# Where the split activations begin in memory, relative to the weights, stage by stage

## The chip, the cores and the metric

One core of one Trainium2 chip runs the program. The metric is the device time in microseconds of that core. The kernel before took 2813.97 us (median of 3 runs, 2809.7 to 2837.8). The execution that was profiled took 2824.21 us, with a span of 2822.4 us from its first to its last instruction.

## The reference, cut to what matters

Two models of two layers each run one after the other on a sequence of 256 tokens of width 1024. The first also carries 256 context tokens, except behind the mixer of its last layer. Every layer is feed-forward, mixer, feed-forward; the mixers are windowed attention, differential attention, retention with dilated attention, and a gated linear attention. In shortened form:

```python
def _swiglu(h, w_gate, w_up, w_down):
    return (jax.nn.silu(h @ w_gate) * (h @ w_up)) @ w_down     # 1024 -> 2816 -> 1024
...
hx = hx + 0.5 * mx[:, 2] * _swiglu(_pre(hx, ...), gate, up, down)   # feed-forward
hx = hx + mx[:, 5] * mixer(_pre(hx, ...))                           # w_in, mixing, w_out
hx = hx + 0.5 * mx[:, 8] * _swiglu(_pre(hx, ...), gate, up, down)   # feed-forward
```

There are eight feed-forwards and four mixers, all in float32. The matrix products with weights make up nearly all of the arithmetic.

## The kernel before, in words

Activations lie transposed: the width is on the 128 partitions, in DT = 8 tiles, and the tokens are the columns (256, or 512 with the context). A float32 product with weights is made from three products in the format float32r. The weight piece (128 x 8 tiles x 128) is loaded into `raw`, ScalarE rounds it to `WH` (L1242), and VectorE writes the rest, raw minus WH, to `WL` (L1579). The activation is split in the same way into a high and a low half. For every weight tile, `three` (L738) issues WH times high (L741), WH times low (L742) and WL times high (L743), all adding into one PSUM bank. Each of these matmuls has its own weight load of 128 columns, which runs beside the matmul before it. So while L741 streams the high half, the WH of L742 is being loaded; beside L742 the WL of L743 is loaded, and beside L743 the WH of the next tile.

The halves lie in two large buffers. `x_all` holds the normalised input of a stage: the high half at element `at`, and the low half at `at` plus 4096 elements (`x_view`, L197). A tile of it is 512 elements. In the stages with 256 columns the feed-forward and the input projection of a mixer read the second half of a tile (`x_scaled`, 256 elements = 1024 bytes further on). `h_all` holds the hidden activation of a feed-forward in the same way, with 22 tiles (`h_view`, L218). The rows of `raw`, `WH` and `WL` are 16384 bytes each and that of `x_all` is 33280 bytes, all multiples of 512, and the allocation brings `h_all` onto the same remainder by 512 bytes (`skew` is there for that). A weight tile is 512 bytes. With `at` = 0 every streamed operand therefore begins on the same remainder by 512 bytes as every weight tile, and `at` shifts it from there: 4 bytes for each element.

Three tuples say what `at` is in each stage. `NORM_X` has it for each of the 13 norms, which stand ahead of: feed-forward 0, attention mixer, feed-forward 1 (first layer of the first model), feed-forward 2, differential mixer, feed-forward 3 (second layer), feed-forward 4, retention mixer, feed-forward 5, feed-forward 6, linear-attention mixer, feed-forward 7 (second model), and the output. `MIX_X` has it for what the four mixers hand to their output projection, and `FFN_H` for the hidden activation of the eight feed-forwards. Feed-forwards 0 to 2 and the first mixer have 512 columns, and so have the four key and value iterations of the differential mixer; all else has 256.

A feed-forward is an "up" stage of 1056 matmuls and a "down" stage of 528. The input projections of the mixers have 288, 192 + 384, 672 and 576, the output projections 192 each, which makes 15552 matmuls in all: 5616 with 512 columns and 9936 with 256. SP loads the weights four pieces ahead, and the order of the stages is fixed. The halves are written by ScalarE (high: L1319, L1386, L1333) and VectorE (low: L1732, L1795, L1746).

Of the kernel before, what the change touches and what calls it, by code (L numbers as in the profile page):

```python
# [31 lines left out]
S = 256  # L32
D = 1024
DT = D // P
# [118 lines left out]
def build(nc, A):  # L153
    ctx = ExitStack()
    with ctx:
# [40 lines left out]

        def x_view(at, low):  # L197

            at += DT * 2 * S if low else 0
            return x_all[:, at:at + DT * 2 * S].rearrange("p (k n) -> p k n", k=DT)  # L200

        NORM_X = (0, 0, 0, 0, 0, 112, 112, 112, 112, 112, 112, 112, 0)
        MIX_X = (0, 112, 112, 112)
        FFN_H = (0, 0, 0, 368, 368, 368, 368, 368)
        x_high = lambda at: x_view(at, False)
        x_low = lambda at: x_view(at, True)


# [90 lines left out]
        def add(g):  # L299
            g.s0 = state["scaled"]  # L300
            if g.kind == "up" and g.scale:
                state["scaled"] += g.iters
            g.p0, g.e0, g.r0, g.a0 = state["p0"], state["e0"], state["r0"], state["a0"]
            state["p0"] += g.n * g.iters
            if g.kind == "res":
                state["r0"] += 4 * g.iters
            else:
                state["e0"] += g.iters
            if g.ada is not None:
                state["a0"] += g.iters  # L310
            gemms.append(g)
            steps.append(("gemm", g))
            return g

        def x_in(at):
            return lambda k, t: (x_high(at)[:, k, 0:t], x_low(at)[:, k, 0:t])
# [8 lines left out]
        def norm(t, weight, shift=None, mode="split"):  # L325
# [4 lines left out]
            n["mul0"] = state["mul"]  # L330
            n["x"] = NORM_X[n["i"]]
            n["c0"] = S if t == S else 0
# [23 lines left out]
        def at(name, d):  # L356

            return A[name][bass.ds(d, 1), :, :, :].rearrange("o p k n -> (o p) k n")

        def ffn(n, t, gate, wg, wu, wd, ada=((KH, None),)):  # L360
            ready, hid0, i0 = (lambda k: (n_low, n["h0"] + k + 1)), state["hid"], 0
            h_at = FFN_H[hid0 // FT]
            for iters, tile in ada:
# [31 lines left out]
        def out_proj(w, t, m, gate):  # L395
            return add(Gemm("res", 2, DT, t, lambda i, _, b: at(w, i * 4 + b),
                            x_in(MIX_X[m]), mix_ready[m], gate=gate))

# [319 lines left out]
        def _(pe):  # L718
# [400 lines left out]
            def gla_low():  # L1119

                pe.wait_ge(gs["wsplit"], 1)
                for k in range(DT):
                    nc.tensor.matmul(bank[4][:, 0:S], a_wh[:, k, :], x_high(MIX_X[3])[:, k, S:2 * S], start=(k == 0), stop=False)
                    nc.tensor.matmul(bank[4][:, 0:S], a_wh[:, k, :], x_low(MIX_X[3])[:, k, S:2 * S], start=False, stop=False)
                    last = nc.tensor.matmul(bank[4][:, 0:S], a_wl[:, k, :], x_high(MIX_X[3])[:, k, S:2 * S], start=False, stop=(k == DT - 1))
                last.then_inc(gs["low"], 1)
# [96 lines left out]
        def _(act):  # L1223
# [172 lines left out]
            def dil_step(n):  # L1396
# [12 lines left out]
                if o is not None:  # L1409
                    act.wait_ge(l_sem["o_turned"], o + 1)  # L1410
                    nc.scalar.activation(x_high(MIX_X[2])[:, 4 + o, 0:S], bank[7][:, 0:S], ACTF.Copy).then_inc(l_sem["o_high"], 1)

# [35 lines left out]
            def pair_high(p):  # L1448
                act.wait_ge(g_sem["o_done"], 3 * p + 3)
                nc.scalar.activation(x_high(MIX_X[0])[:, p, :], bank[6 + p % 2], ACTF.Copy).then_inc(g_sem["x_high"], 1)  # L1450

# [733 lines left out]
```

## Time and profile before

| what | value |
|---|---|
| median of 3 runs | 2813.97 us (2809.7 to 2837.8) |
| the profiled execution, its span | 2824.21 us, 2822.4 us |
| TensorE busy | 2740.4 us, 97% of the span, 17468 matmuls |
| VectorE, ScalarE, GpSimd busy | 63%, 43%, 7% |
| mean granted TensorE clock | 0.991 |
| chain that ended last | 88% TensorE |

The busy time of an engine is the time in which at least one of its instructions runs. Matmuls overlap in the records, since each one's end is modelled and lies behind the start of the next, so the cost of one in a dense stretch is the distance from start to start (here called the pitch): the length of the stretch by the number of matmuls in it.

### The profile page before, as it was taken

To read this page: it belongs to the slowest core of one execution; us is meant where nothing else is said; L and a number is where in the kernel's file an instruction comes from. 1 tells how busy PE (TensorE), PEld (TensorE's weight loads), DVE (VectorE), ACT (ScalarE), POOL (GpSimd) and SP (SyncE) were. 2 spreads that over 40 slices of the span, in tenths; PEclk is the share of its full clock that TensorE was granted. 3 is DMA by queue.
4 is the path that set the end of the run, shared out by engine and by line. 5 is a ranking of instruction groups with operands and counts; after the bars stand their busy time and mean duration, and the time that the engine had idled before them with its cause. 6 is when DMAs were issued, how large, how long until landed. Compare 5 with 4: busy or idle time off the path is not lost.

```text
span 2822.4 us, 45969 instructions
## 1 busy us (share of the span) xinstructions
PE 2740.4 (97%) x17468; PEld 2420.4 (86%) x17468; DVE 1768.1 (63%) x2690; ACT 1206.6 (43%) x1808; POOL 200.2 (7%) x246
## 2 busy tenths in 40 slices
PE   7999999999999999999998999999989999999998
PEld 5888886678888888888875999999879999988998
DVE  5977344847874287732548655667666666667665
ACT  4322223833222243322326555654446556544563
POOL 0100011010100100001100101002000000000001
PEclk9999999999999999999999999999989999999999
DMA  8666323025664346633330565666426566653564
GB/s 307 209 197 186 95 88 90 2 75 170 209 191 122 113 155 192 187 90 98 102 104 16 161 183 181 191 187 218 121 90 183 182 181 192 181 167 97 174 189 137
DMA packets 118687, 424.31 MB, mean 150 GB/s; under 512 B 13280, under 2 KB 14320, under 8 KB 117408
## 3 DMA queue, kind: packets, MB, share of 16 engines
q1 hardware_dynamic: 98528, 353.41, 40.5%
q0 software_dynamic: 18992, 68.09, 8.0%
q8 instruction: 88, 1.44, 0.2%
q10 hardware_dynamic: 1040, 1.05, 0.1%
q14 instruction: 39, 0.32, 0.0%
HBM read 421.45 MB, written 1.05 MB: 150 GB/s over the span
## 4 chain that ended last, share of the span: by engine, by line
PE 88%; DVE 6%; ACT 2%; issue 2%; DMA 1%; SPq 0%; DVEq 0%; ACTq 0%
PE bank L741 28%; PE bank L742 28%; PE bank L743 28%; DVE WL L1579 1%; ACT WH L1242 1%; DMA f_nat<-in_ada_n 1%; DVE rstd L1775 1%; DVE g_max L1878 1%; DVE d_small L1940 1%; PE bank L874 1%; PE bank L982 0%; PE bank L959 0%; DVE g_p L1898 0%; DVE tn L1785 0%; DVE x_all L1795 0%
## 5 line engine op out<-in xcount | busy, mean ns | idle before, releaser
L741 PE MATMUL bank<-x_all,WH 128*128 128x256 f32 (+1 forms) x3776 | 1217.8, 322 | 23.4 <-DVE x_all L1795 6.2
L742 PE MATMUL bank<-x_all,WH 128*128 128x256 f32 (+1 forms) x3776 | 1205.5, 319 | 0.0
L743 PE MATMUL bank<-x_all,WL 128*128 128x256 f32 (+1 forms) x3776 | 1205.2, 319 | 0.0
L1579 DVE TENSOR_TENSOR WL<-raw,WH 128x1024 fp32r<-128x1024 f32 (+1 forms) x664 | 806.9, 1218 | 626.2 <-ACT WH L1242 623.0
L1242 ACT ACTIVATE WH<-raw 128x1024 fp32r<-128x1024 f32 (+1 forms) x664 | 682.3, 1035 | 796.5 <-PE bank L743 782.3
L741 PEld LDWEIGHTS bank<-x_all,WH 128*128 128x128 f32 x3776 | 716.6, 190 | 86.0 <-issue 12.1
L742 PEld LDWEIGHTS bank<-x_all,WH 128*128 128x128 f32 x3776 | 715.9, 190 | 54.7 <-issue 3.1
L743 PEld LDWEIGHTS bank<-x_all,WL 128*128 128x128 f32 x3776 | 713.8, 189 | 52.8
L743 PE MATMUL bank<-h_all,WL 128*128 128x256 f32 (+1 forms) x1408 | 450.9, 320 | 0.0
L741 PE MATMUL bank<-h_all,WH 128*128 128x256 f32 (+1 forms) x1408 | 450.9, 320 | 0.0
L742 PE MATMUL bank<-h_all,WH 128*128 128x256 f32 (+1 forms) x1408 | 450.9, 320 | 0.0
L1626 DVE CUSTOM_DVE_ANT_0 sq<-a_rows,c_all 128x1024 bf16<-128x1024 f32 x248 | 303.0, 1222 | 4.3
L741 PEld LDWEIGHTS bank<-h_all,WH 128*128 128x128 f32 x1408 | 265.8, 189 | 20.5
L742 PEld LDWEIGHTS bank<-h_all,WH 128*128 128x128 f32 x1408 | 265.0, 188 | 20.5
L743 PEld LDWEIGHTS bank<-h_all,WL 128*128 128x128 f32 x1408 | 264.3, 188 | 20.8
L702 POOL TENSOR_TENSOR sq<-sq 128x256 f32<-128x256 f32 (+1 forms) x72 | 89.8, 1247 | 1638.7 <-ACT sq L1328 1175.6
L1746 DVE TENSOR_TENSOR h_all<-tn,h_all 128x256 f32 (+3 forms) x176 | 91.9, 522 | 104.5 <-ACT h_all L1333 104.5
L1254 ACT ACTIVATE sg<-bank 128x512 f32<-128x512 f32 (+1 forms) x88 | 47.9, 545 | 251.7 <-PE bank L743 251.7
L691 POOL DMA_DIRECT2D a_rows<-in_ada_t x124 | 66.0, 533 | 664.9 <-DVE a_acc L1626 631.8
L1333 ACT ACTIVATE h_all<-tn 128x256 f32 (+3 forms) x176 | 86.5, 491 | 57.5 <-DVE tn L1678 56.3
L1678 DVE TENSOR_TENSOR tn<-sg,bank 128x256 f32<-128x256 f32 (+1 forms) x176 | 91.0, 517 | 19.4 <-PE bank L743 18.4
L1699 DVE SCALAR_TENSOR_TENSOR xT<-bank,gates,xT 128x256 f32<-128x256 f32 x80 | 35.8, 480 | 84.2 <-PE bank L743 84.2
(318 smaller groups left out, 1620.6 us busy)
## 6 DMA issues: line engine op xcount, KB each, us to landing
a_rows<-in_ada_t POOLq DMA_DIRECT2D x124, 512.0 KB, 4.1
raw<-in_ffn_w_gate SPq DMA_DIRECT2D x88, 512.0 KB, 3.6
raw<-in_ffn_w_up SPq DMA_DIRECT2D x88, 512.0 KB, 4.3
raw<-in_ffn_w_down SPq DMA_DIRECT2D x64, 512.0 KB, 3.6
raw<-in_ffn_pre_w_gate SPq DMA_DIRECT2D x44, 512.0 KB, 3.6
raw<-in_ffn_pre_w_up SPq DMA_DIRECT2D x44, 512.0 KB, 4.3
raw<-in_ffn_post_w_gate SPq DMA_DIRECT2D x44, 512.0 KB, 3.6
raw<-in_ffn_post_w_up SPq DMA_DIRECT2D x44, 512.0 KB, 4.4
```

Of the source, the lines that this page charges most:

```text
L691: pool.dma_start(a_rows[:, t % 2, :].rearrange("p (k n) -> p k n", k=DT), at("ada_t", t)).then_inc(ada_in[t % 2], 16)
L702: nc.gpsimd.tensor_tensor(sq[:, 0, 0:t], sq[:, 0, 0:t], sq[:, 1, 0:t], ALU.add).then_inc(sq_sum, 2 if k == 1 else 1)
L741: nc.tensor.matmul(o, WH[:, j % 4, k, :], high, start=start, stop=False)
L742: nc.tensor.matmul(o, WH[:, j % 4, k, :], low, start=False, stop=False)
L743: return nc.tensor.matmul(o, WL[:, j % 4, k, :], high, start=False, stop=stop)
L1242: nc.scalar.activation(WH[:, b, 0:g.depth(j), :], raw[:, b, 0:g.depth(j), :], ACTF.Copy).then_inc(h_done, 1)
L1254: nc.scalar.activation(sg[:, b // 2, 0:t], bank[b][:, 0:t], ACTF.Silu).then_inc(act_bank, 1)
L1333: nc.scalar.activation(h_view(g.h_at, False)[:, bass.ds(f, 1), 0:g.t], hf[:, half:half + 1, 0:g.t], ACTF.Copy).then_inc(hid_high, 1)
L1579: nc.vector.tensor_tensor(WL[:, b, 0:d, :], raw[:, b, 0:d, :], WH[:, b, 0:d, :].bitcast(F32), ALU.subtract).then_inc(split_done, 1)
L1626: nc.vector.tensor_tensor_reduce(out=a_prod[:, :], in0=a_rows[:, b % 2, :], in1=c_all[:, half, :], scale=1.0, scalar=0.0, op0=ALU.mult, op ...
L1678: nc.vector.tensor_tensor(hf[:, half, 0:t], sg[:, half, 0:t], bank[b][:, 0:t], ALU.mult).then_inc(dve_bank, 1)
L1746: nc.vector.tensor_tensor(h_view(g.h_at, True)[:, bass.ds(f, 1), 0:g.t], hf[:, half:half + 1, 0:g.t], h_view(g.h_at, False)[:, bass.ds(f, ...
```

## The change

Each of the three tuples gets other values. For `x_all` an entry is now a pair, the first for the high half and the second for the low half, so that the two can begin at different remainders. `x_all` keeps its 128 spare elements and `h_all` its 368. No instruction is added, removed or moved; only addresses differ.

```diff
         def x_view(at, low):
 
-            at += DT * 2 * S if low else 0
+            at = DT * 2 * S + at[1] if low else at[0]
             return x_all[:, at:at + DT * 2 * S].rearrange("p (k n) -> p k n", k=DT)
 
-        NORM_X = (0, 0, 0, 0, 0, 112, 112, 112, 112, 112, 112, 112, 0)
-        MIX_X = (0, 112, 112, 112)
-        FFN_H = (0, 0, 0, 368, 368, 368, 368, 368)
+        NORM_X = ((0, 16), (0, 32), (0, 48), (16, 64), (32, 64), (48, 64), (0, 16), (16, 32), (16, 32), (0, 48), (0, 32), (0, 32), (0, 0))
+        MIX_X = ((0, 32), (32, 64), (16, 32), (0, 32))
+        FFN_H = (8, 4, 12, 4, 12, 20, 28, 60)
```

In bytes from the remainder of the weights: 112 elements were 448, and 368 elements were 1472, which is 448 by 512 as well. The new entries of `x_all` are 0, 64, 128, 192 and 256 bytes. Those of `h_all` are 32, 16, 48, 16, 48, 80, 112 and 240 bytes, the same for both halves.

## Rows read from the trace of the kernel before

**Rows 1.** The page: busy time of the engines, with shares and instruction counts.

```profile
PE 2740.4 (97%) x17468; PEld 2420.4 (86%) x17468; DVE 1768.1 (63%) x2690; ACT 1206.6 (43%) x1808; POOL 200.2 (7%) x246
```

**Rows 2.** The page: the chain that ended last, by engine, then by line.

```profile
PE 88%; DVE 6%; ACT 2%; issue 2%; DMA 1%; SPq 0%; DVEq 0%; ACTq 0%
PE bank L741 28%; PE bank L742 28%; PE bank L743 28%; DVE WL L1579 1%; ACT WH L1242 1%; DMA f_nat<-in_ada_n 1%; DVE rstd L1775 1%; DVE g_max L1878 1%; DVE d_small L1940 1%; PE bank L874 1%; PE bank L982 0%; PE bank L959 0%; DVE g_p L1898 0%; DVE tn L1785 0%; DVE x_all L1795 0%
```

**Rows 3.** Windows: stages with 512 columns (stretch, length, TensorE busy and count, clock).

```profile
40.70:280.10 239.40, 239.40 (x1056) 1.00 0.65 199
280.10:399.80 119.70, 119.70 (x529) 1.00 0.33 97
...
1237.00:1356.60 119.60, 119.60 (x529) 1.00 0.33 97
```

**Rows 4.** Windows: stages with 256 columns (up to three matmuls overlap the edges).

```profile
1578.50:1702.90 124.40, 124.40 (x1057) 1.00 0.57 175
1702.90:1765.10 62.20, 62.20 (x531) 1.00 0.60 183
1765.10:1886.90 121.80, 121.80 (x1062) 1.00 0.63 191
1886.90:1946.80 59.90, 59.90 (x531) 1.00 0.60 189
...
2238.50:2300.70 62.20, 62.20 (x531) 1.00 0.61 184
2300.70:2425.80 125.10, 125.10 (x1063) 1.00 0.62 186
2425.80:2488.00 62.20, 62.20 (x531) 1.00 0.62 186
...
2749.70:2809.50 59.80, 59.80 (x530) 1.00 0.48 146
```

**Rows 5.** Timeline: 256 columns, offset 0; 24 pitches lie between these two starts.

```profile
1384.87 0.28 PE L741 MATMUL bank<-x_all,WH 128*128 128x256 f32 x1
...
1387.75 0.28 PE L741 MATMUL bank<-x_all,WH 128*128 128x256 f32 x1
```

**Rows 6.** Timeline: 256 columns, feed-forward 4, 24 pitches between the first two and last two.

```profile
1775.29 0.28 PE L741 MATMUL bank<-x_all,WH 128*128 128x256 f32 x1
...
1778.12 0.28 PE L741 MATMUL bank<-x_all,WH 128*128 128x256 f32 x1
...
1780.86 0.28 PE L741 MATMUL bank<-x_all,WH 128*128 128x256 f32 x1
...
1783.58 0.28 PE L741 MATMUL bank<-x_all,WH 128*128 128x256 f32 x1
```

**Rows 7.** The chain in order of time: four float32 matmuls of 512 columns.

```profile
455.53 1.72 PE bank L848 x4
```

**Rows 8.** Groups by line and form: weight loads of 128 and of 64 columns.

```profile
L797 PEld LDWEIGHTS bank<-ident 128*128 128x128 f32 x352 | 40.5, 192 | 4.5 <-issue 4.4
L996 PEld LDWEIGHTS bank<-g_pt,g_vn 128*64 128x64 f32 x320 | 17.5, 136 | 5.3 <-issue 3.8 <-ACT g_pt L1429 0.3
```

**Rows 9.** Groups by line and form: who writes the weights and the halves.

```profile
L1579 DVE TENSOR_TENSOR WL<-raw,WH 128x1024 fp32r<-128x1024 f32 x600 | 745.7, 1245 | 503.0 <-ACT WH L1242 500.1 <-DVE mods L1617 0.2
...
L1333 ACT ACTIVATE h_all<-tn 128x256 f32 x100 | 41.0, 410 | 11.3 <-DVE tn L1678 10.1
L1386 ACT ACTIVATE x_all<-tn,mods 128x256 fp32r<-128x256 f32 x88 | 39.8, 502 | 50.0 <-DVE tn L1785 50.0
```

**Rows 10.** Waits of TensorE, longest in total: us, times, longest.

```profile
PE bank L741 <- DVE x_all L1795: 6.2, 12, 0.8
```

## The prediction

> **What bounds the kernel now.** I read the page first. TensorE is busy 97% of the span [rows 1], and the chain that ended last runs through it for 88%, 84% of that in the three lines of `three` [rows 2]. So the time is, to a first approximation, 15552 matmuls times their pitch, and 1 ns on each is 15.6 us. VectorE, ScalarE and the loads feed TensorE without being its bound: the largest wait of TensorE for a written half is 6.2 us in total [rows 10], and VectorE itself idles 503 us ahead of its weight splits [rows 9].
>
> Next comes the pitch of each stage, from the windows. With 512 columns, all at offset 0, it is 239.4 us by 1056, or 226.7 ns, in an up stage, and the same within 0.1% in the downs, both the first and the third (119.6 us by 528: 226.5) [rows 3]. At the full clock of 2.4 GHz (granted clock 1.00 in these rows) 512 columns take 213.3 ns, so each matmul carries 13.3 ns on top. With 256 columns, which take 106.7 ns, two levels come out at offset 448: 124.4 us by 1056 and 62.2 by 528 (117.8 ns) in feed-forwards 3, 5 (down) and 6, and 59.8 or 59.9 us by 528 (113.3 ns) in the downs of 4 and 7 [rows 4]. The surcharge is 11.1 ns in one case and 6.7 in the other. The one stage with 256 columns at offset 0, the query projection of the differential mixer, has 2.88 us for 24, or 120.0 ns: a surcharge of 13.3 again [rows 5].
>
> Two things follow. The surcharge at offset 0 is the same with 256 columns and with 512, so it goes with each weight load rather than with each column. And the offset is not all that sets it. Within feed-forward 4, at one address pattern, 24 pitches take 2.83 us and 3 us later 2.72 us [rows 6]: the stage falls from the one level to the other and stays there. Offset 448 has two stable rhythms, 117.8 and 113.3, and a disturbance chooses. I read this as the stream and the load of the next weights colliding somewhere in memory, the offset setting which rhythms can lock in. This is inferred from pitches alone; no row shows a collision.
>
> **The change part by part.** Nothing is issued, removed or moved, no wait is added and no queue is passed. The writers of the halves get other addresses. An activation of 256 columns takes 410 or 502 ns [rows 9]; a write off the 64-byte raster could cost nothing or, as a bound, 10% of 0.5 us on each of the 8 tiles that a stage waits for at its start: 12 stages by 8 by 0.05 us is 4.8 us. It could gain nothing, since the data must be written either way. I take 0, as the writers' own waits stand beside TensorE's work.
>
> What remains is the price of the new offsets (0, 64, 128, 192 and 256 bytes for x, 16 to 240 for h), none of which but 0 occurs in a dense stretch of the trace. It is bounded from both sides. Upwards, no steady stretch is worse than a surcharge of 13.3 ns, so I take that as the upper end. Downwards, four float32 matmuls of 512 columns take 1.72 us [rows 7], 430 ns each; taken as two passes, 512 columns take 215. For 256 columns the load is the lower end: 128 columns against 64 are 192 against 136 ns [rows 8], 56 ns for 64 columns, 112 ns for a full load, so 113.3 is nearly the floor. For a moved operand I take the better level measured away from 0, a surcharge of 6.7; for one left at 0, the 13.3 of offset 0. In terms of the three matmuls: high carries two, low one. Each term is a count times a difference to the profiled execution.
>
> - 512 columns, all operands moved: the up stage of feed-forward 2 (1056), keys and values of the differential mixer (384), three downs (1584). 3024 times 6.7 ns: 20.2 us gained.
> - 512 columns, only low moved: the up stages of feed-forwards 0 and 1, the attention mixer in and out, 2592, a third of them low. 864 times 6.7: 5.8 us gained.
> - The query projection: 192 times 6.7, 1.3 us gained.
> - 256 columns now at 117.8, high and low both moved, none to 0: feed-forwards 3 and 5, the down of 6, the output projection of the differential mixer, 3888 times 4.5: 17.4 us gained.
> - 256 columns whose high goes from 448 back to 0: the up stages of feed-forwards 4 and 7, the linear-attention mixer in and out, 2880 now mostly at 113.3. Two thirds times 6.7: 12.8 us lost. The up stage of feed-forward 6 comes out even (704 lose 2.2 ns, 352 gain 4.5).
> - The downs of 4 and 7 and the retention mixer are at the good level already: 0.
>
> The sum is 20.2 + 5.8 + 1.3 + 17.4 - 12.8 = 31.9 us. Against the profiled execution, 2824.2, this is 2792.3. The median of the runs is 10.2 us below that execution, and I count the gain against it: 2782 us. That is generous by a few us if the median run had more stages at 113.3 than the profiled one, which would also explain why the three runs spread over 28 us: all of feed-forward 3, 5 and 6 between its two levels is worth 4752 times 4.5, or 21 us.
>
> Where would a gained microsecond go next? The 256-column pieces would stay at 24 times 113, 2.7 us, which the present supply of weights already carries without gaps in the downs of 4 and 7 [rows 4]. The 512-column pieces take 5.4 us now. The cover holds.
>
> A rule of the Trainium skill speaks against the change. What the rows show is that 256 columns at full clock take 120.0 ns at offset 0 and 113.3 or 117.8 at 448 [rows 4 to 6], with the same instructions. The skill, "TensorE: Matmul & The Clock Gate", section "Step-by-step: what each phase is for", says that TensorE reads its memory through two independent ports, one for the streamed operand and one for the weights. By that, addresses relative to each other would not matter and the change would give 0 instead of 32 us. The difference between the offsets speaks against it, the two levels at one offset speak partly for it, and so it backs the second rival.
>
> **The rivals.**
>
> 1. *Half the way is the whole way* (chance 0.12). A high and a low at different offsets may keep any bad rhythm from locking in, the high left at 0 included. Then every matmul comes to the surcharge of 6.7: 5616 times 6.7, 4944 times 4.5 and 192 times 6.7, together 37.6 + 22.2 + 1.3 = 61 us, 2753 us. For it: the rhythm is shared by all three matmuls, since the pitch of 24 is even. Against it: nothing in the trace has mixed offsets.
> 2. *The offsets do nothing* (0.22). The rhythm is chosen by how a stage starts; the offset in bytes matters little, and 120 against 117.8 is one more rhythm. Then the 512-column stages keep 226.7 and the rest draws its levels anew: 2814 us, with up to 22 us either way. For it: the fall within feed-forward 4. Against it: 512 columns show one level in all stages, and offset 0 never shows 113.3 in steady state.
> 3. *The high at 0 pulls the low with it, and the hidden halves do no better off the raster* (0.13). Its place is the 256-column stages that leave 448. The up stages of 4 and 7 and the linear mixer go to 120.0: 2880 times 6.7, 19.3 us; the up of 6: 1056 times 2.2, 2.3 us; the downs of 3, 5 and 6: 1584 times 2.2, 3.5 us; those of 4 and 7: 1056 times 6.7, 7.1 us. With 512 columns, nothing improves. Together 32 us: 2846 us. It decides from the point at which a 256-column stage with its high at 0 reads 119 ns or more in its dense part and the 512-column stages still read 226.
>
> **How the numbers follow.** The forecast has 0.53, and 2782 us. Its own range runs from 2760 (moved operands of 512 columns near the lower end, 4 ns better on 5616) to 2806 (half of the 512-column gain and half of the 117.8 stages fail). The range of 8 in 10 reaches from 2742, a little past the first rival for surcharges below 6.7, to 2828, which takes in the second rival but for its worst draws and leaves most of the third out. This kernel can tell 1% from no change, 28 us. Below 2786: 0.7 of the forecast and all of the first rival, about 0.50. Above 2842: most of the third rival and a rest, 0.14. Between: 0.36.
>
> **What would show it.** In the windows of the profile after: the downs of feed-forwards 0 to 2 below 119.6 us, 116.1 by the forecast (528 times 220.0); the up stage of 2 at 232 us instead of 239.5; those of 0 and 1 at 237; the down of 3 at 59.9 instead of 62.2; the ups of 4 and 7 two or three us longer in their dense parts. Within a triple with its high at 0, the two high matmuls should be slower than the low one; if all three pitches move together, the first or the third rival is nearer. The forecast is wrong if the 512-column stages stay at 226.7, as they carry 26 of the 32 us, or if a 256-column stage comes out over 120. The counts of instructions and the waits of TensorE should be as before.

## The result, and the profile after

The changed kernel takes 2868.49 us (median of 4 runs, 2864.05 to 2871.37) against 2819.19 us for the kernel before (4 runs, 2809.7 to 2837.8): 1.015 times, with a 95% interval of 1.0116 to 1.0184. It is slower, and the interval lies wholly above 1. The forecast was 2782 us, and the range ended at 2828.

The profiled execution after has a span of 2867.9 us where the one before had 2822.4. The page's first and fourth parts look as they did [rows 1, 2]; TensorE is busy 44.5 us longer with the same number of matmuls. Its weight loads, which run beside them, are busy 17.8 us longer; VectorE, ScalarE and GpSimd stay within 2 us.

```profile
PE 2784.9 (97%) x17468; PEld 2438.2 (85%) x17468; DVE 1769.9 (62%) x2690; ACT 1205.0 (42%) x1808; POOL 200.2 (7%) x246
...
PE 89%; DVE 6%; ACT 2%; issue 2%; DMA 1%; SPq 0%; DVEq 0%; ACTq 0%
```

The wait for the written halves [rows 10] is the same to the tenth, and the writers themselves take what they took (409 and 501 ns for an activation of 256 columns, where 410 and 502 stood). So the writers' new addresses cost TensorE nothing:

```profile
PE bank L741 <- DVE x_all L1795: 6.2, 12, 0.8
```

The stages tell where the time went. These are windows of the kernel after (stretch, length, TensorE busy and count, clock, DMA share, GB/s). The order is: the up and down stages of feed-forwards 0, 1 and 2 with 512 columns, then with 256 the up and down of 3, the up and down of 4, and the down of 6.

```profile
41.50:286.50 245.00, 245.00 (x1056) 1.00 0.62 194
286.50:409.70 123.20, 123.20 (x530) 1.00 0.32 95
641.90:883.70 241.80, 241.76 (x1056) 1.00 0.60 183
883.70:1006.10 122.40, 122.40 (x530) 1.00 0.34 103
1016.10:1262.60 246.50, 246.50 (x1057) 1.00 0.54 162
1262.60:1385.80 123.20, 123.20 (x530) 1.00 0.32 94
1608.70:1734.70 126.00, 126.00 (x1057) 1.00 0.56 173
1734.70:1794.50 59.80, 59.80 (x530) 1.00 0.61 190
1794.50:1922.90 128.40, 128.40 (x1063) 1.00 0.60 182
1922.90:1985.30 62.40, 62.40 (x530) 1.00 0.60 183
2465.70:2525.60 59.90, 59.90 (x530) 1.00 0.62 191
```

Every 512-column stage is slower. The ups take 245.0, 241.8 and 246.5 us where they took 239.4 or 239.5, the downs 122.4 to 123.2 where they took 119.6 or 119.7 [rows 3]. From first to last matmul, all 512-column stages that read `x_all` lose 18.3 us and the three downs 9.6 us. With 256 columns [rows 4] the picture is mixed: the downs of 3 and 6 fell from 62.2 to 59.8 and 59.9, that of 4 rose from 59.9 to 62.4, and its up rose from 121.8 to 128.4. Together the stages that read `x_all` lose 15.6 us there and the downs 0.3. The four parts make 43.9 of the 45.5 us.

Pitches below are those of the dense part of a stage, read from the starts in the timeline as in [rows 5, 6]. Two of the kernel after, 24 pitches apart, in the down of feed-forward 0: 5.60 us, 233.3 ns each, where 226.7 stood.

```profile
297.70 0.39 PE L741 MATMUL bank<-h_all,WH 128*128 128x512 f32 x1
...
303.30 0.39 PE L741 MATMUL bank<-h_all,WH 128*128 128x512 f32 x1
```

### The profile page after: what moved, and what is told of

It reads as the page before. It is cut to its first block, busy times and chain, and to the rows that moved or that the text cites. A ratio compares the mean times of both kernels' runs of the same rounds, so it can differ in the third digit from the quotient of the medians.

```text
span 2867.9 us, 45989 instructions
## 1 busy us (share of the span) xinstructions
PE 2784.9 (97%) x17468; PEld 2438.2 (85%) x17468; DVE 1769.9 (62%) x2690; ACT 1205.0 (42%) x1808; POOL 200.2 (7%) x246
## 4 chain that ended last, share of the span: by engine, by line
PE 89%; DVE 6%; ACT 2%; issue 2%; DMA 1%; SPq 0%; DVEq 0%; ACTq 0%
PE bank L741 28%; PE bank L742 28%; PE bank L743 28%; DMA f_nat<-in_ada_n 1%; DVE WL L1579 1%; ACT WH L1242 1%; DVE g_max L1878 1%; DVE rstd L1775 1%; DVE d_small L1940 1%; PE bank L874 1%; PE bank L982 0%; DVE g_p L1898 0%; PE bank L959 0%; DVE tn L1785 0%; DVE x_all L1795 0%
## 5 line engine op out<-in xcount | busy, mean ns | idle before, releaser
L1251 ACT ACTIVATE sg<-sg 128x256 f32<-128x256 f32 x88 | 36.8, 418 | 127.3 <-DVE sg L1670 127.2
```

## The experiments

All kernels differ from the changed one in the three tuples alone, unless it is said otherwise. *Distance* is the offset of a half in bytes from the remainder of the weights; 112 is 28 elements. In tuples, elements stand as in the code.

**One part alone: x_all.**

```diff
-        FFN_H = (8, 4, 12, 4, 12, 20, 28, 60)
+        FFN_H = (0, 0, 0, 368, 368, 368, 368, 368)
```

> The x_all offsets of the change with the hidden halves back at their old offsets. Read from the two traces, stage by stage: the stages that read x_all take 18.3 us more with 512 columns and 15.6 us more with 256. If each stage's pitch is set by its own offsets alone, those 34 us stay here and the down stages return to 119.6 us (512 columns) and 59.8 or 62.2 (256): about 1.012 times the kernel before, some 2853 us. If the hidden halves off the 64-byte raster were the cause, it comes back to the kernel before: 1.000, 2819 us.

Measured: 2851.82 us, 1.0107 times before (1.0058 to 1.0156). The up of feed-forward 0 keeps its 245.1 us and the down after it returns to 119.7:

```profile
40.80:285.90 245.10, 245.09 (x1057) 1.00 0.63 195
285.90:405.60 119.70, 119.70 (x530) 1.00 0.33 97
```

**The other part alone: the hidden halves.** `NORM_X` and `MIX_X` have their old values as equal pairs.

> The hidden halves' offsets of the change with x_all as before. If each stage's pitch is set by its own offsets, the three downs with 512 columns keep 123.0, 122.1 and 123.0 us instead of 119.6 (9.6 us in all) and the five with 256 columns come out even: 1.003 to 1.004, some 2829 us. If off-raster hidden halves are the cause of the whole loss, 1.015, 2862 us.

Measured: 2833.84 us, 1.0053 times (1.0024 to 1.0082). The up is back at 239.5, the down stays at 123.2:

```profile
40.80:280.30 239.50, 239.49 (x1057) 1.00 0.65 199
280.30:403.50 123.20, 123.20 (x530) 1.00 0.31 94
```

The two parts add up (1.1% and 0.5%), and a stage's pitch goes with its own entry. Neither is the cause alone. There are exceptions with 256 columns: the down of feed-forward 3, at 16 bytes, reads 116.7 ns here and 113.3 in the change, and the up of 3 reads 113.3 at the very offsets at which the kernel before read 117.8.

**Undo the 512-column entries.**

```diff
+        NORM_X = ((0, 0), (0, 0), (0, 0), (0, 0), (32, 64), (48, 64), ...)
+        MIX_X = ((0, 0), (32, 64), (16, 32), (0, 32))
+        FFN_H = (0, 0, 0, 4, 12, 20, 28, 60)
```

> The change without its entries for the 512-column stages ahead of the differential mixer (feed-forwards 0 to 2 and the attention mixer), which go back to offset 0. If the pitch is each stage's own, these stages return to 226.7 ns a matmul and give back 27.4 us of the 44: 2841 us, 1.006 to 1.008 times the kernel before. If the time is set by how rhythms carry over from stage to stage, the 256-column stages change as well, by 5 us or more in sum.

Measured: 2840.74 us, 1.0076 times (1.0054 to 1.0098): 27.8 us less than the change, as the stages' sum said. All 512-column stages at distance 0 read 226.7 ns. Of the others the down of feed-forward 3 differs (116.7 ns where the change had 113.3) and the linear mixer slightly (117.8 where the change read mostly 116.7), so carry-over between stages is worth some 2.5 us here. The five microseconds that were named as its sign are not reached.

**Equal halves on the raster, another distance in each stage.**

```diff
+        NORM_X = ((16, 16), (32, 32), (48, 48), (64, 64), (96, 96), (0, 0), (16, 16), (32, 32), (32, 32), (48, 48), (64, 64), (64, 64), (0, 0))
+        MIX_X = ((80, 80), (16, 16), (32, 32), (64, 64))
+        FFN_H = (16, 32, 64, 16, 32, 48, 64, 0)
```

> Both halves of x_all at one offset, multiples of 64 bytes, another in each stage; the hidden halves on the raster too. 512 columns: 64, 128, 192, 256, 384 bytes (x), 64, 128, 256 (hidden). 256 columns: 0, 64, 128, 192, 256 (x), 64, 128, 192, 256, 0 (hidden). If unequal halves are what costs, every 512-column stage reads 226.7 ns a matmul here and no 256-column stage reads over 120. If the distance from the weights is what counts, equal halves included, the 512-column stages differ among each other and some read 229 to 233 ns. x_all and the hidden buffer must then agree at the same distance, as 64 and 128 bytes occur in both.

The up and the down of feed-forward 0 (both 64 bytes), the up of 1 (192), the up and the down of 2 (both 256), and, with 256 columns, the downs of 6 (256) and 7 (0):

```profile
40.80:282.60 241.80, 241.77 (x1056) 1.00 0.64 197
282.60:403.50 120.90, 120.90 (x530) 1.00 0.32 97
633.40:879.90 246.50, 246.48 (x1057) 1.00 0.60 180
1012.60:1252.10 239.50, 239.47 (x1056) 1.00 0.55 167
1252.10:1371.80 119.70, 119.70 (x530) 1.00 0.33 97
2455.00:2518.30 63.30, 63.30 (x529) 1.00 0.61 182
2789.30:2852.60 63.30, 63.30 (x529) 1.00 0.45 138
```

Equal halves are no cure: 228.9 ns at 64 bytes and 233.3 at 192, and the kernel took 2867.60 us (one run). The two buffers agree at the same distance, but for 192 bytes with 256 columns, where the hidden halves read 113.3 and x_all mostly 117.8; and 256 bytes behaves as 0, in both widths. The pitch counts the distance by 256 bytes. The up and the down of feed-forward 0 read the same 228.9 ns while the loads moved 197 and 97 GB/s, so the traffic of the loads is not what sets it.

**The weights moved instead of the stream.** A pad of 64 bytes ahead of `raw` moves `raw`, `WH`, `WL` and the hidden halves; x_all stays. x_all has equal halves: at 16 elements in feed-forwards 0, 1, 4, the attention and the linear mixer, at 0 in the up of feed-forward 2, at 32 in those of 5 and 6. The hidden halves have other offsets as well.

```diff
+        w_pad = sb("w_pad", [P, 16])
         raw = sb("raw", [P, 4, DT, P])
```

> raw, WH, WL and the hidden buffer lie 64 bytes further on, x_all where it was. If the distance between stream and weights is what counts, x_all at 64 bytes now behaves as at 0: 226.7 ns with 512 columns in feed-forwards 0 and 1 and the attention mixer, 120.0 with 256 in feed-forward 4 and the linear mixer; feed-forward 2's up stage, at 0, behaves as at 192 and reads 233.3; the up stages of feed-forwards 5 and 6, at 128, read 117.8 as at 64. If the absolute place of the stream counts, x_all at 64 bytes keeps the 228.9 and 117.8 it had in e3_equal_map, and feed-forward 2 keeps 226.7 at 0.

The ups of feed-forwards 0, 1 and 2:

```profile
40.90:280.30 239.40, 239.40 (x1056) 1.00 0.65 199
628.30:867.80 239.50, 239.45 (x1056) 1.00 0.61 184
997.60:1244.00 246.40, 246.40 (x1056) 1.00 0.54 162
```

So 226.7 at 64 bytes with the weights moved by 64, and 233.3 where the stream stayed; all other predicted values came too (120.0, 117.8). The kernel took 2853.67 us (one run). The distance between stream and weights counts, not the place of either. That it is TensorE's two reads that disturb each other is the likely reading, and it is not shown: no row shows a collision, and the engines that write `raw`, `WH` and `WL` had their addresses moved as well.

**Off the raster.** Two kernels with equal halves, other distances in every stage.

> Equal halves, another distance in each stage, multiples of 16 bytes: 512 columns 80, 208, 112, 144, 224, 176 (x), 96, 160, 240 (hidden); 256 columns 112, 96, 80, 144, 160, 176 (x), 112, 208, 224, 176, 128 (hidden). If the pitch is a function of the distance alone, 112 bytes reads 113.3 ns in both buffers, as the down of feed-forward 6 did after the change, and 176 the same in both. If 0 is the best distance for 512 columns, none of the nine reads under 226.7. If the two writers' off-raster writes mattered, the stages would have new waits of TensorE for them.

```diff
+        NORM_X = ((20, 20), (52, 52), (28, 28), (36, 36), (56, 56), (28, 28), (24, 24), (20, 20), (20, 20), (36, 36), (40, 40), (40, 40), (0, 0))
+        MIX_X = ((44, 44), (44, 44), (20, 20), (40, 40))
+        FFN_H = (24, 40, 60, 28, 52, 56, 44, 32)
```

> As before with distances between the multiples of 16 bytes: 512 columns 4, 8, 24, 40, 56 bytes (x), 252 (attention out), 120, 248, 184 (hidden); 256 columns 120, 8, 104, 116, 240, 4 (x), 116, 24, 120, 108, 96 (hidden). If the line of 16 bytes is the grain, 4 and 8 bytes behave as 0 (226.7 and 120.0) and 116 and 120 as 112 (113.3). If every 4 bytes count, they differ from these by a nanosecond or more.

```diff
+        NORM_X = ((1, 1), (2, 2), (6, 6), (10, 10), (14, 14), (30, 30), (2, 2), (26, 26), (26, 26), (29, 29), (60, 60), (60, 60), (0, 0))
+        MIX_X = ((63, 63), (1, 1), (26, 26), (60, 60))
+        FFN_H = (30, 62, 46, 29, 6, 30, 27, 24)
```

Measured: 2873.41 and 2905.09 us, one run each; the second is the slowest kernel of this study.

With the kernels above and below, the pitch in ns by distance, both halves at the same one and full loads (several values where several rhythms were seen):

| distance mod 256 | 0 | 4 | 8 | 16 | 24 | 48 | 64 | 80 | 104 | 108 |
|---|---|---|---|---|---|---|---|---|---|---|
| 512 columns | 226.7 | 237.9 | 233.3 | 231.7 | 234.2 | 233.3 | 228.9 | 231.1 | | |
| 256 columns | 120.0 | 123.3 | 116.7 | 113.3, 116.7, 118.7 | 120.0 | 118.3 | 117.8 | 118.3, 120.0 | 120.0, 130.0 | 120.0 |

| distance mod 256 | 112 | 116 | 128 | 144 | 176 | 192 | 208 | 240 |
|---|---|---|---|---|---|---|---|---|
| 512 columns | 226.7, 231.1 | | 232.3 | 233.3 | 233.3 | 233.3 | 234.7 | 236.7 |
| 256 columns | 113.3 | 121.7 | 118.7 | 118.7 | 119.3 | 113.3, 117.8 | 119.2 | 117.1 |

The line of 16 bytes is not the grain: every 4 bytes count. Nothing reads under 226.7 or 113.3, and both are 17/16 of the columns' time (213.3 and 106.7 ns). The two widths have different maps: at 8 bytes 256 columns read 116.7, less than at 0, and 512 columns 233.3, more than at 0. A good distance can be narrow: 112 bytes reads 113.3 with 256 columns, 108 and 116 read 120.0 and 121.7. From the first kernel, the up of feed-forward 1 at 112 bytes, the down of 2 at 240 bytes, the up and the down of 3, both at 112, and the down of 4 at 208:

```profile
639.40:878.80 239.40, 239.40 (x1056) 1.00 0.61 185
1259.10:1384.00 124.90, 124.90 (x529) 1.00 0.31 93
1608.00:1727.80 119.80, 119.80 (x1057) 1.00 0.60 182
1727.80:1787.60 59.80, 59.80 (x530) 1.00 0.63 189
1916.00:1978.90 62.90, 62.90 (x530) 1.00 0.61 182
```

From the second, the up of feed-forward 0 at 4 bytes, and a stretch of the up of 5 at 104 bytes (130.0 ns, by its starts), where the retention mixer read 120.0 at the same distance:

```profile
40.70:292.00 251.30, 251.26 (x1057) 1.00 0.62 190
2200.00:2280.00 80.00, 80.00 (x618) 1.00 0.57 170
```

**Halves apart.**

```diff
+        NORM_X = ((0, 28), (28, 64), (0, 64), (28, 92), (28, 28), (28, 52), (28, 92), (0, 28), (0, 28), (28, 64), (52, 116), (52, 116), (0, 0))
+        MIX_X = ((0, 16), (0, 64), (0, 28), (52, 116))
+        FFN_H = (50, 54, 58, 50, 54, 58, 8, 16)
```

> High and low at different distances, each of them one that reads 226.7 (512 columns) or 113.3 or 120.0 (256) with equal halves. 512 columns in bytes: (0, 112), (112, 256), (0, 256), (112, 368). 256 columns: (112, 208), (112, 368), (0, 112), (112, 256), (208, 464). If the distance counts by 256 bytes, (0, 256) reads 226.7 and (112, 368) 226.7 and 113.3 as equal halves do. If each matmul had its price by its own distance, all 512-column stages read 226.7, (112, 208) and (208, 464) read 113.3 and (0, 112) 117.8. If a step in distance between neighbouring matmuls costs by itself, the mixed pairs read more: over 228 with 512 columns. The hidden halves sample 200, 216 and 232 bytes with 512 columns and 200, 216, 232, 32 and 64 with 256.

The ups of feed-forwards 0 (0, 112 bytes), 1 (0, 256) and 2 (112, 368), and of 3 (112, 208) with 256 columns:

```profile
41.00:286.30 245.30, 245.30 (x1057) 1.00 0.63 194
640.20:879.60 239.40, 239.40 (x1056) 1.00 0.60 185
1012.90:1252.30 239.40, 239.40 (x1056) 1.00 0.55 167
1596.40:1723.20 126.80, 126.77 (x1056) 1.00 0.56 172
```

Measured: 2865.34 us (one run). A pair whose halves are 256 bytes apart behaves as an equal pair: 226.7 and 226.7, with 256 columns 120.0 for (0, 256), 113.3 for (112, 368) and 119.2 for (208, 464). The expectation took 208 bytes for a distance of 113.3 ns; the row above has it at 119.2. Other pairs can cost more than either of their parts: (0, 112) reads 232.2 with 512 columns and mostly 122.2 with 256, and (112, 208) reads 120.0 where 112 alone reads 113.3 and 208 alone 119.2. That is no rule. In the change (0, 192) reads 228.9 with 512 columns, just the mean of two matmuls at 226.7 and one at 233.3, and (0, 128) reads 116.7 to 117.8 with 256 columns, less than 0 alone (120.0) and 128 alone (118.7). So the price is not one of single matmuls that adds up, and a mixed pair has to be measured.

**The lows at their highs.**

```diff
+        NORM_X = ((0, 0), (0, 0), (0, 0), (16, 16), (32, 32), (48, 48), (0, 0), (16, 16), (16, 16), (0, 0), (0, 0), (0, 0), (0, 0))
+        MIX_X = ((0, 0), (32, 32), (16, 16), (0, 0))
```

> The change with each low half of x_all moved to the offset of its high half; the hidden halves as in the change. From the pitches by distance: with 512 columns the up stages of 0, 1 and 2 gain 5.6, 2.3 and 4.5 us and the attention mixer 2.8; with 256 the up stage of 3 gains 1.5 to 6 and those at distance 0 (6, 7, the linear mixer) lose 7 together. Sum 9 to 14 us less than the change: 2856 us, 1.013 times the kernel before. If unequal halves were the whole trouble, it would come to within 0.5% of the kernel before.

Measured: 2859.05 us, 1.0134 times (1.0103 to 1.0164), 9.4 us less than the change. The price list by distance forecast the kernel to 3 us. Net, unequal halves are a fifth of the trouble, and the distances chosen are the other four. The fifth is a difference. In the profiles, first to last matmul, four stages or mixers with 512 columns (the ups of 0 to 2 and the attention mixer) gain 15.5 us by equal halves, while the ups of 6 and 7, whose pairs (0, 192) and (0, 128) become (0, 0), lose 4.5, and the downs of 3 and 5, whose entries did not change, lose 3.7 by another rhythm (118.7 and 120.0 ns).

**Half the weight load.** In the up stages of feed-forwards 1, 2, 4 and 7, `three` uses half of each weight tile; x_all at distances 0, 192, 0 and 112 bytes.

```diff
+                    nc.tensor.matmul(o[0:64], WH[:, j % 4, k, 0:64], high, start=start, stop=False)
+                    nc.tensor.matmul(o[0:64], WH[:, j % 4, k, 0:64], low, start=False, stop=False)
+                    return nc.tensor.matmul(o[0:64], WL[:, j % 4, k, 0:64], high, start=False, stop=stop)
```

> The three matmuls of the up stages of feed-forwards 1, 2, 4 and 7 load only 64 of the 128 weight columns and write only 64 partitions (half of that product is left out); their streams are whole. Distances: feed-forward 1 at 0 and 2 at 192 bytes (512 columns), 4 at 0 and 7 at 112 bytes (256). With full loads these four read 226.7, 233.3, 120.0 and 113.3 ns. If the whole surcharge over the columns' time comes from the loads (13.3, 20.0, 13.3, 6.7), it halves: about 220, 223, 113 and 110. If one sixteenth of the columns' time (13.3 and 6.7 ns) is the stream's own and only the rest comes from the load, they read 226.7, 230, 117 and 113.3.

Measured: 230.0, 232.6, 113.3 and 116.7 ns. In this order, windows of the ups of 1 and 4:

```profile
628.90:871.80 242.90, 242.89 (x1056) 1.00 0.59 182
1767.20:1888.70 121.50, 121.50 (x1063) 1.00 0.64 192
```

The matmuls also write only 64 partitions of their output, so this edit changes two things. The kernel took 2814.02 us (one run). Both theories missed. The halved load made two of the four stages slower (226.7 to 230.0, 113.3 to 116.7) and one reach the 113.3 it had never reached at distance 0. It neither halves the surcharge nor leaves it alone: what is loaded and written changes which distances fit. That the time never falls under 17/16 held here too, with half the load, which speaks for that sixteenth being the stream's own, but does not show it.

**Two candidates for a better version.** First 512 columns at 0 and 256 columns at 112 bytes:

```diff
+        NORM_X = ((0, 0), (0, 0), (0, 0), (0, 0), (0, 0), (28, 28), (28, 28), (28, 28), (28, 28), (28, 28), (28, 28), (28, 28), (0, 0))
+        MIX_X = ((0, 0), (28, 28), (28, 28), (28, 28))
+        FFN_H = (0, 0, 0, 28, 28, 28, 28, 28)
```

> 512 columns at distance 0 as before the change, every 256-column stage but the query projection with both halves at 112 bytes. If the single rhythm of 113.3 ns that the down of feed-forward 6 showed there in three kernels belongs to the distance, all these stages read 113.3: against the profile before, 4944 matmuls gain 4.5 ns, 22 us, and the runs scatter less: about 2800 us against 2818, 0.993. If the rhythm is drawn anew at each start, the stages show 117.8 as well and the time is that of before, 2818.

Measured: 2804.29 us, 0.9926 times before (0.9899 to 0.9953). All 256-column stages but the query projection read 113.3 in their dense parts, as the up and down of feed-forward 3 show:

```profile
1576.20:1696.00 119.80, 119.80 (x1057) 1.00 0.60 182
1696.00:1755.80 59.80, 59.80 (x530) 1.00 0.62 189
```

Its ten runs lie within 2801.64 and 2805.95 us; twelve of the kernel before in the same comparison lie between 2807.13 and 2840.39. Then 112 bytes everywhere, `(28, 28)` and `28` in every entry but the output's, which is not read by a matmul:

> Both halves at 112 bytes in every stage, 512 columns included. Against e8_28_for_256 only the query projection gains (120.0 to 113.3 ns on 192 matmuls, 1.3 us) and the 512-column stages keep 226.7: 0.992 to 0.993 times the kernel before. If 226.7 at 112 bytes was luck of one stage, the 512-column stages show other pitches.

Measured: 2814.67 us, 0.9984 times (0.9961 to 1.0006), no difference that these runs can tell. The profiled execution shows every 512-column stage at 231.1 ns, as here the up of feed-forward 0, where one stage of the off-raster map had read 226.7 at the same distance:

```profile
40.90:285.00 244.10, 244.10 (x1057) 1.00 0.64 195
```

Its twelve runs spread from 2809.49 to 2832.36, and the profiled one is the slowest of them. So 112 bytes has one rhythm with 256 columns and two with 512. An estimate from these pitches: 4.4 ns on 5616 matmuls are 24.7 us, about the spread of the runs, so faster runs probably had 226.7 in some stages. The first version is the best kernel of this study.

## Why the prediction was wrong

Term by term, between the two profiled executions, from first to last matmul of each stage (plus is a loss, minus a gain):

| term of the sum | forecast us | measured us |
|---|---|---|
| 512 columns, all operands moved | -20.2 | +17.2 |
| 512 columns, only low moved | -5.8 | +10.7 |
| query projection | -1.3 | 0.0 |
| 256 columns at 117.8, both halves moved | -17.4 | -3.7 |
| 256 columns, high back to 0 | +12.8 | +12.6 |
| up of feed-forward 6 | 0 | +0.1 |
| downs of 4 and 7, retention mixer | 0 | +6.9 |

- *TensorE's pitch sets the time, and each nanosecond is 15.6 us.* Right: 43.9 of the 45.5 us lie in the stages of `three`, nearly all of it as longer pitches.
- *No steady stretch is worse than a surcharge of 13.3 ns, so this is the upper end*, and a moved operand of 512 columns goes from 13.3 to 6.7. This is the step that failed. The trace before had 512 columns at one distance only, and I took its 13.3 ns for the worst since 256 columns had less. It was the best: 14 kernels have no 512-column stage under it, and the change brought 15.6 to 20.0. The two terms in which 512 columns gain (20.2 and 5.8) came out as losses of 27.9 us. The error was to compare surcharges in ns across widths. As a share, 226.7 and 113.3 are both 17/16 of the columns' time, and the trace before already had both numbers.
- *The surcharge goes with each load.* Wrong for the same reason: at distance 0, 256 columns carry 6.7 ns over 17/16 and 512 columns none. Halving the load did not halve it.
- *A moved operand takes the better level, 6.7 ns.* Wrong for most distances, with 256 columns too. Of the 256-column stages, only the downs of feed-forwards 3 and 6 reached 113.3; they gained 2.3 us each of the 2.4 forecast. The downs of 4 and 5 read 118.3, the ups of 3 and 5 read 119.3 and 117.8.
- *The downs of 4 and 7 and the retention mixer are at the good level already: 0.* Wrong by 6.9 us. Their distances changed too, and they went from 113.3 to 118.3, 117.1 and 117.8 ns. By the forecast's own rule a moved operand could only gain or stay.
- *The high at distance 0 loses.* Right in size: 12.6 us for 12.8, the up of 7 at the 117.8 ns that two highs at 120.0 and a low at 113.3 would give, the up of 6 even. (The sign that was given, two or three us more in each of these ups, did not fit the term, which was 4.7 each; 6.5 and 5.9 came.) The mechanism was not right, so the size is in part luck. By the starts over some 200 triples, the pitches behind high, low and high are 120.0, 122.0 and 118.0 ns in the up of 4, 118.2, 117.7 and 117.5 in that of 6, and 116.7, 119.1 and 117.6 in that of 7: no low is faster than its highs by 6.7 ns, and in two of three the low is the slowest. At 128 bytes alone 256 columns read 118.7, not 113.3.
- *The two levels at one offset are rhythms chosen by a disturbance.* The levels are confirmed: 192 bytes reads 113.3 or 117.8 in many stages. What chooses is not shown. The best version, whose stages read one rhythm each, holds its ten runs within 4.3 us.
- *The writers' addresses cost 0, at most 4.8 us.* Right: the waits are unchanged.
- *Four float32 matmuls of 512 columns take 1.72 us* [rows 7], the lower end for 512 columns. The kernel issues two matmuls at L848, and each stands in the trace as two records 0.43 us apart. So one takes 0.86 us, and 215 ns is a quarter of it, if that is four passes. No dense stage with float32r came near 215.
- *The rivals.* The first took the mixing of distances for a help; with 512 columns it was mostly a cost, with 256 sometimes a help, and it never brought the 6.7 ns. The second (the offsets do nothing) is refuted. The third had the right sign and its 256-column mechanism in one stage (the up of 4 at 120.0), but held the 512-column stages at 226.7, so it had the wrong place. No rival let 512 columns get worse, and that was three fifths of the loss.

The rule of the Trainium skill that I weighed ("TensorE: Matmul & The Clock Gate", "Step-by-step: what each phase is for": two independent read ports for stream and weights) would have made the weights' move of 64 bytes invisible. The runs show 226.7 against 228.9 or 233.3 ns by it, so the trace does not agree, and here the measurement decides against independence in that sense.

What stays open: why the pitch repeats after 256 bytes and 4 bytes matter within it, whether it is the load of the weights or another access to them that meets the stream, what a rhythm is inside TensorE, and which event picks 226.7 or 231.1 at 112 bytes. These runs show that the distance decides which pitches a stage can have, not how.

## What to carry to other kernels

Before calling a number a worst case, set it as a ratio to the ideal time and look at every width; a surcharge that is the same ratio at every width may be a floor, as it was here. Where matmuls run dense, the distance of the streamed operand from the stationary one moved the pitch by 5% with 512 columns (226.7 to 237.9 ns) and by 15% with 256 (113.3 to 130.0); it can be mapped in a few runs by giving each stage its own distance, and it must be mapped for each width. Prefer a distance with a single rhythm to one with a lucky one. Keep the halves of a split operand at the same distance unless the pair has been measured: five of the seven mixed pairs with 512 columns read more than either part alone.

## What the runs showed that I had not expected

- A float32r matmul of N columns never came under N times 17/16 of the clock's time: 226.7 and 113.3 ns, averaged over eight weight tiles, over 14 kernels and all distances, with full or half loads. Whether float32 pays it depends on its number of passes, which no run shows: with four passes, the 0.86 us of a float32 matmul [rows 7] are 215 ns each, and it would not.
- The pitch depends on the distance between stream and weights by 256 bytes: 0 and 256 read the same, and the pair (112, 368) reads what 112 reads.
- A change of 4 bytes costs up to 11.2 ns a matmul (226.7 to 237.9 with 512 columns, from 0 to 4 bytes).
- The scatter of the kernel before (2806.65 to 2838.26 us over 17 runs) is probably for the most part a draw of rhythms in the 256-column stages. This is an estimate, as only one of its executions was profiled: that one took 2824.2 us, its 4752 matmuls at 117.8 ns would give back 21 us at 113.3, and the 3168 of feed-forwards 4 and 7, mostly at 113.3, would cost 14 at 117.8; so draws reach from 2803 to 2838. With x_all at the very same offsets, the up of feed-forward 3 took 124.4 us in one profile [rows 4] and 119.8 in that of the kernel with only the hidden halves changed:

```profile
1588.80:1708.60 119.80, 119.80 (x1057) 1.00 0.60 182
```

The best version, whose stages read one rhythm each, has no such scatter.
